# Expert 31's up matrix ahead of the second half of expert 30's down matrix, in a one-core hybrid layer with 32 experts

## What is computed

```
def clamped_swiglu(a, u):
    a = jnp.minimum(a, SWIGLU_LIMIT)
    u = jnp.clip(u, -SWIGLU_LIMIT, SWIGLU_LIMIT)
    return a * jax.nn.sigmoid(SWIGLU_ALPHA * a) * (u + 1.0)
...
    logits = (t @ router_w + router_b).astype(jnp.float32)
    top_v, top_i = lax.top_k(logits, TOP_K)
    gates = jax.nn.softmax(top_v, axis=-1)
...
    def expert_block(inp):
        tok, gt, e = inp
        xb = t_pad[tok]
        hid = clamped_swiglu(xb @ w_gate[e] + b_gate[e], xb @ w_up[e] + b_up[e])
        yb = hid @ w_down[e] + b_down[e]
        return (yb * gt[:, None].astype(yb.dtype)).astype(t.dtype)
```

## Time and profile before

| | us |
|---|---|
| median of 3 runs | 1059.69 (1058.49 to 1059.8) |
| the profiled execution's own time | 1057.99 |
| its span, first to last instruction | 1056.2 |
| TensorE busy | 1019.8 (97%) |
| VectorE busy | 228.7 (22%) |
| ScalarE busy | 143.8 (14%) |

### The profile page before, as it was taken

One profiled execution on the slowest core, in us unless ns is written; L12 is line 12 of the kernel. 1 busy time (PEld: TensorE's weight loads), 2 busy tenths in 40 slices (PEclk: granted clock), 3 DMA queues, 4 the chain that ended last, 5 costly groups with the idle time before them and its releaser, 6 DMA issues.

```text
span 1056.2 us, 12142 instructions
## 1 busy us (share of the span) xinstructions
PE 1019.8 (97%) x5116; PEld 448.6 (42%) x5116; DVE 228.7 (22%) x495; ACT 143.8 (14%) x348; POOL 30.6 (3%) x50
## 2 busy tenths in 40 slices
PE   8999999999999999999999999999999999999997
PEld 7888764333333333332333333333333333233332
DVE  5453652111111111111111112211111111111112
ACT  3312331111111111101110011111111111011102
POOL 1230100000000000000000000000000000000000
PEclk9999999999999999999999999999999999999999
DMA  9894889999999999999999999999999999999995
GB/s 314 274 412 191 267 314 357 432 426 436 431 429 430 433 432 431 431 434 432 431 431 434 431 429 430 431 433 430 431 428 434 432 432 429 434 426 426 428 419 238
DMA packets 40587, 426.21 MB, mean 404 GB/s; under 512 B 6986, under 2 KB 19411, under 8 KB 24036
## 3 DMA queue, kind: packets, MB, share of 16 engines
q1 hardware_dynamic: 38516, 424.12, 95.9%
q10 hardware_dynamic: 2032, 1.53, 0.6%
HBM read 424.59 MB, written 1.05 MB: 403 GB/s over the span
## 4 chain that ended last, share of the span: by engine, by line
PE 69%; DMA 29%; ACT 1%; DVE 0%; issue 0%; SPq 0%; POOL 0%; DVEq 0%; POOLq 0%; ACTq 0%
PE bank L1215 29%; DMA ring<-in_moe_w_up 18%; PE bank L1266 15%; DMA ring<-in_moe_w_gate 11%; PE bank L1195 4%; PE bank L1187 4%; PE bank L871 3%; PE bank L886 2%; PE bank L1061 2%; PE bank L1049 1%; PE bank L1003 1%; PE bank L1257 1%; PE bank L1135 1%; PE bank L964 1%; PE bank L1069 1%; PE bank L1235 1%
## 5 line engine op out<-in xcount | busy, mean ns | idle before, releaser
L1215 PE MATMUL bank<-ring,arena 128*64 128x512 f32 x1980 | 444.5, 601 | 24.5 <-DMA ring<-in_moe_w_up 20.7
L1215 PEld LDWEIGHTS bank<-ring,arena 128*64 128x64 f32 x1980 | 141.3, 138 | 297.3 <-issue 253.6
L1266 PE MATMUL bank<-ring,arena 128*64 128x512 f32 x1024 | 226.8, 595 | 1.5 <-issue 1.5
L1266 PEld LDWEIGHTS bank<-ring,arena 128*64 128x64 f32 x1024 | 71.5, 137 | 151.7 <-issue 150.1
L1663 DVE COPY arena<-bank 128x512 f32<-128x512 f32 x32 | 22.1, 692 | 326.1 <-PE bank L1266 326.1
L756 ACT ACTIVATE arena<-arena 128x512 f32<-128x512 f32 x32 | 20.1, 630 | 451.4 <-DVE arena L1650 451.4
L1195 PE MATMUL bank<-arena 64*128 64x512 f32 x256 | 72.0, 640 | 0.9 <-DVE arena L1663 0.9
L1187 PEld LDWEIGHTS bank<-arena 128*128 128x128 f32 x480 | 58.8, 196 | 22.8 <-issue 22.8
L1657 DVE TENSOR_SCALAR arena<-bank 128x512 f32<-128x512 f32 x32 | 22.1, 692 | 209.2 <-PE bank L1215 209.2
L767 ACT ACTIVATE arena<-bank 128x512 f32<-128x512 f32 x32 | 19.1, 597 | 336.3 <-PE bank L1257 336.3
L1187 PE MATMUL bank<-arena 128*128 128x128 f32 x480 | 64.5, 288 | 0.0
(11 more groups left out here) (281 smaller groups left out, 514.6 us busy)
## 6 DMA issues: line engine op xcount, KB each, us to landing
ring<-in_moe_w_down SPq DMA_DIRECT2D x25, 4096.0 KB, 28.3
ring<-in_moe_w_gate SPq DMA_DIRECT2D x24, 4096.0 KB, 24.7
ring<-in_moe_w_up SPq DMA_DIRECT2D x24, 4096.0 KB, 27.5
ring<-in_moe_w_down SPq DMA_DIRECT2D x10, 2048.0 KB, 16.6
ring<-in_moe_w_gate SPq DMA_DIRECT2D x9, 2048.0 KB, 21.4
ring<-in_moe_w_up SPq DMA_DIRECT2D x9, 2048.0 KB, 15.1
ring<-in_w_in SPq DMA_DIRECT2D x12, 1024.0 KB, 11.9
ring<-in_moe_w_gate SPq DMA_DIRECT2D x8, 1024.0 KB, 17.9
```

What stands on the lines that cost most here:

```text
L1215: ins = mm(b[h * SL:(h + 1) * SL, :], (xA[pp], xB)[q][:, k, par * SL:(par + 1) * SL], columns(unit_at(m, kt), h), start=False, stop=kt == ...
L1266: ins = mm(bank[6][h * SL:(h + 1) * SL, :], hidT[:, kt % 4, (kt // 4) * SL:(kt // 4 + 1) * SL], unit_at(2, kt)[:, h * 512:(h + 1) * 512], ...
```

## The change

Four edits, all around the last two experts:

- SP skips the second half of down of expert 30 at its place, and asks for it (line 446 of the changed kernel) behind the five pieces of up of expert 31, ahead of down of expert 31. It goes to the slot that it had before.
- TensorE multiplies the first half of down of expert 30 at its old place, then gate and up of expert 31, and only then the second half. Its weights, the hidden rows of expert 30, have a buffer of their own (`hidT30`).
- `scatter(30, 0)` and `scatter(30, 1)` move from either side of up of expert 31 to ahead of the first and behind the second of the eight row groups of its down. The transposes of `selG` go to bank 7 in tile 31, since bank 6 still holds half a sum.
- VectorE's copy of expert 30's result to `y_s` moves from the end of tile 30 to the end of tile 31, behind the last step of its hidden rows.

```diff
@@ SP @@
                         for rows, done in zip(HALVES, (landed[s], landed2[s])):
+                            if (e, m) == (NE - 2, 2) and rows is HALVES[1]:
+                                s30 = s
+                                continue
                             sp.dma_start(slot(s)[:, rows, :], piece_src(e, m, rows)).then_inc(done, 16)
                     elif isinstance(e, int) and e == NE - 1:
                         for c, rows in enumerate(map(slice, LAST_PIECES[m], LAST_PIECES[m][1:])):
                             sp.dma_start(slot(s)[:, rows, :], piece_src(e, m, rows)).then_inc(w_landed[LAST_AT[m] + c - 1] if c else landed[s], 16)
+                        if m == 1:
+                            sp.dma_start(slot(s30)[:, HALVES[1], :], piece_src(NE - 2, 2, HALVES[1])).then_inc(landed2[s30], 16)
@@ ScalarE @@
-                nc.scalar.activation(selGT[par], bank[6][:, 0:SEQ], ACT.Copy).then_inc(selGT_ok, 1)
+                b = bank[7] if isinstance(n, int) and n == NE - 1 else bank[6]
+                nc.scalar.activation(selGT[par], b[:, 0:SEQ], ACT.Copy).then_inc(selGT_ok, 1)
...
+                dst = hidT30 if isinstance(n, int) and n == NE - 2 else hidT
+                nc.scalar.activation(dst[:, :, :].rearrange("p c n -> p (c n)"), bank[4][:, :], ACT.Copy).then_inc(hidT_ok, 1)
@@ TensorE @@
+                def down(kts, hid, rows_at, here):
+                    for kt in range(KT)[kts]:
+                        here(2, kt)
+                        for h in range(2):
+                            ins = mm(bank[6][h * SL:(h + 1) * SL, :], hid[:, kt % 4, (kt // 4) * SL:(kt // 4 + 1) * SL],
+                                     rows_at(2, kt)[:, h * 512:(h + 1) * 512], start=kt == 0, stop=kt == KT - 1)
+                        if kt == KT - 1 or (kt + 1 in FIRST_PIECES[2] if first else kt == 3):
+                            ins.then_inc(d_ps if kt == KT - 1 else unit_used, 1)
...
-                if last:
-                    scatter(n - 1, 0, 1 - par)
                 hidden(1, bank[5], u_ok, u_ps)
...
                 if last:
-                    scatter(n - 1, 1, 1 - par)
+                    down(slice(4, 8), hidT30, rows_30, arrived_30)
                 pe.wait_ge(hid_ok, n + 1)
...
+                if last:
+                    scatter(n - 1, 0, 1 - par)
+                    pe.wait_ge(yd_ok, n)
+                    down(slice(0, 2), hidT, unit_at, arrived)
+                    scatter(n - 1, 1, 1 - par)
+                    down(slice(2, 8), hidT, unit_at, arrived)
+                elif isinstance(n, int) and n == NE - 2:
+                    down(slice(0, 4), hidT30, unit_at, arrived)
+                else:
+                    down(slice(0, 8), hidT, unit_at, arrived)
@@ VectorE @@
+                for of in {NE - 2: (), NE - 1: (NE - 2, NE - 1)}.get(n, (n,)) if isinstance(n, int) else (n,):
+                    dve.wait_ge(d_ps, of + 1)
+                    if not first:
+                        dve.wait_ge(scat[1], of)
+                    copy(y_s, bank[6][:, :]).then_inc(yd_ok, 1)
```

More of the change, by code:

```diff
@@ L148, in build @@
         hidT = cut(10368, 4, P)
+        hidT30 = cut(14272, 4, P)
         y_s = cut(12160, 512)
@@ L766, in tile @@
                     act.wait_ge(d_ps, n)
-                nc.scalar.activation(hidT[:, :, :].rearrange("p c n -> p (c n)"), bank[4][:, :], ACT.Copy).then_inc(hidT_ok, 1)
+                dst = hidT30 if isinstance(n, int) and n == NE - 2 else hidT
+                nc.scalar.activation(dst[:, :, :].rearrange("p c n -> p (c n)"), bank[4][:, :], ACT.Copy).then_inc(hidT_ok, 1)
                 if ahead is not None:
@@ L1197, in scatter, with tile @@
                 ins.then_inc(scat[t], 1)
-            def tile(n, par, first, unit_at, arrived, pp, gathers, scatters, late=None):
+            def tile(n, par, first, unit_at, arrived, pp, gathers, scatters, late=None, rows_30=None, arrived_30=None):
+                def down(kts, hid, rows_at, here):
[6 more added lines that the diff above has]
+                            ins.then_inc(d_ps if kt == KT - 1 else unit_used, 1)
                 def hidden(m, b, free, done):
@@ L1230, in tile @@
                     gate_transposes()
-                else:
+                last = isinstance(n, int) and n == NE - 1
+                if not first and not last:
                     pe.wait_ge(yd_ok, n)
@@ L1234, in tile @@
                 for t in range(NT):
-                    ins = tr(bank[6][:, t * P:(t + 1) * P], selG[:, par, t, :], ident[:, :])
+                    ins = tr(bank[7 if last else 6][:, t * P:(t + 1) * P], selG[:, par, t, :], ident[:, :])
                 ins.then_inc(selT_ps, 1)
@@ L1238, in tile @@
                     pe.wait_ge(list_ok, 1)
-                last = isinstance(n, int) and n == NE - 1
-                if last:
-                    scatter(n - 1, 0, 1 - par)
                 hidden(1, bank[5], u_ok, u_ps)
@@ L1312, in arrived, with rows_30, arrived_30 @@
                             pe.wait_ge(w_landed[u], 48 if u < 8 else 32)
+                    def rows_30(m, kt):
+                        return slot(ring_at(stage, UPE * (k - 1) + m) % RING)[:, kt, :]
+                    def arrived_30(m, kt):
+                        if kt == 4:
+                            pe.wait_ge(landed2[ring_at(stage, UPE * (k - 1) + m) % RING], (2 + UPE * UNROLL // RING) * 16)
                     first = isinstance(n, int) and n == 0
@@ L1319, in experts @@
                          (n + 2, it * (UNROLL // 2) + (k // 2 + 1), k % 2) if ahead else None, not first,
-                         n - LATE if isinstance(n, int) and n in (LATE, LATE + 1) else None)
+                         n - LATE if isinstance(n, int) and n in (LATE, LATE + 1) else None, rows_30, arrived_30)
                     if isinstance(n, int) and n == UNROLL - 1:
```

## The result

Seven executions of the changed kernel took 1061.84 to 1066.05 us, median 1063.83; seven of the kernel before 1058.17 to 1059.80, median 1059.13. The ratio is 1.0045, with a 95% interval of 1.0035 to 1.0056: slower, by 4.7 us between the medians.

What follows compares the result with a forecast made beforehand. TensorE and transfers were both taken as full, the end bounded by the last landing and the work behind it. 2.9 us for the later copy plus 1.5 for the clock, on 1059.69, gave 1064.1 us, range 1061.3 to 1066.3.

Steps and rivals of the forecast that it cites:

- The forecast's floor: At the end: behind a last landing at 1042.8 the copy can't start before 1043.9; reordering gains at most 0.2 us.
- The landings: Expert 31's gate and up land 5.0 us earlier, the moved half at 1032.8; down of expert 31 stays at 1042.8.
- TensorE up to the wait: Gate of expert 31 ends at 1020.42, up at 1028.7; TensorE then waits 4.1 us for the moved half.
- Behind the wait: From the half's landing at 1032.8 to the copy at 1047.0: 14.2 us of work, against 14.0 in the old order.
- The two terms: At the end: 2.9 us for the later copy, plus 1.5 us for a clock fall at the wait, 4.4 in sum.
- the rival with a second fall: Clock falls again after the 1.48 us gap behind the transposes: 2.9 + 3.4, 1066.0 us; counted in the forecast's case.
- two reasons: Behind up of expert 31: decisive landing is 1032.8, not 1030.0; scatters fill no 1.48 us wait, since scatter awaits `hidT_ok`.
- Wait without a fall: Rival: TensorE waits for the moved half but the clock does not fall; 1062.6 us, chance 0.18.
- land early: Rival: the moved half lands out of order, at 1028.7 TensorE doesn't wait; 1059.5 us, not slower, chance 0.11.
- its case: Wait for the moved half and fall of the clock: 1063.3 to 1066.4 us, chance 0.68.

Runs made afterwards that it cites:

- the version at 0.9997: Changed kernel with the moved half in four 0.5 MB pieces and expert 30's first scatter ahead of the wait for hidT_ok: 1058.72 us, ratio 0.9997.
- the second trace: The changed kernel run once more, unaltered, for a closer figure and another trace: 1064.14 us, ratio 1.0050 against the kernel before.
- the pieces: Changed kernel with the moved half asked for in pieces, each waited for by itself: two of 1 MB 1059.86 us, four of 0.5 MB 1059.46 us.
- the still later half: Changed kernel with the moved half asked for behind the first 1 MB of expert 31's down: 1066.16 us, ratio 1.0072.
- the scatters alone: Kernel before with only expert 30's two scatters moved among expert 31's down products, its down and copy at their old place: 1061.81 us, ratio 1.0028.
- the filler matmuls: Changed kernel with ten idle matmuls between up of expert 31 and the wait for the moved half: 1061.51 us, ratio 1.0028.

## Why the prediction was right

It named 1064.1 us in 1061.3 to 1066.3; the median is 1063.83. That the two are 0.3 us apart is partly luck: the forecast added 4.4 us to a median of 1059.69, and the measured rise was 4.7 over a median of 1059.13. What stands on record is the rise, and its two terms. Step by step:

- **What bounds the end.** The forecast's floor (copy not before 1043.9, with the last landing at 1042.8) was not contradicted, and not reached by any new version either. No version's ratio is clearly below 1; the lowest is 0.9997. But the last weights landed 6.3 us ahead of the copy in the changed kernel, and 1.6 us ahead of it in the version at 0.9997 (asked for at 1023.94, 19.5 us to landing, copy at 1045.04), where the forecast's floor is 1.1. That the stream's end, and not the order of the products, would stop a better order is argued and not shown.
- **The landings.** It had the moved half at 1032.8 and up's fifth row group at 1025.0; they came at 1032.5 and 1025.07. The last piece of down came at 1042.4, where 1042.8 was forecast. SP's queue cost nothing visible: the half was asked for 27.6 us ahead.
- **TensorE up to the wait.** Gate's end was put at 1020.42 (the selection's transposes start at 1020.44), up's at 1028.7 (32.52 less 3.79 is 28.73), the wait at 4.1 against 3.79.
- **Behind the wait.** 14.2 us from landing to copy were forecast; with the clock held up it is 14.47, the two row groups between the scatters taking 1.87 (1040.34 to 1042.21) instead of 1.73 and the half 3.58 instead of 3.5. With the low clock it is 16.17.
- **The two terms.** Traces give 2.9 for landing and order (4.61 less 1.70) and 1.70 for the clock in the profiled execution; 2.9 and 1.5 were forecast. That the clock falls at all had a chance of 8 in 10 in the forecast, and it fell in all three traces with a wait of 3.8 us or more. The clock's term was given 0 to 1.7 for one low stretch. In the second trace it was 2.55, above that bound but inside the 3.4 of the rival with a second fall. The rule of the Trainium skill (TensorE: Matmul & The Clock Gate, "HAM oscillation"), a wait for a transfer and a next burst that starts at half rate, agrees with two of the three traces that have the long wait (granted clock 0.50 from within the wait on). In the first one the burst's first 0.5 to 0.9 us were still at 1.00, and then it was 0.50 too.
- **Why the gain didn't come.** The text named two reasons. The later landing of the half has its runs in the pieces and in the still later half. That scatters among the down products don't fill the wait for `hidT_ok`, since they stand behind it, has one too: with the first scatter moved ahead of that wait, it is filled (0.5 us). What the text didn't price by itself is the scatters' move: it puts 2.1 us of work behind the landings (the scatters alone, by its trace).
- **The rivals.** Wait without a fall is what the filler matmuls make: 1061.51 against the 1062.6 named (the medians of before differ by 1 us; as a ratio 1.0028 against 1.0027). The half did not land early: up's pieces ahead of it, then the half, in the order of asking. A second fall is in none of the three traces with the long wait; its place as the dear case is taken by the one longer low stretch.
- **A slip in the sum.** 1059.69 plus 2.9, 3.4 and 0.3 is 1066.3, and not the 1066.4 that the text gives as the upper end of its case. The stated range isn't touched by it.

The size that no term explains is small: the scatters alone lose 0.9 us more by the ratio than in their trace.

## What to carry to other kernels

When a stream of transfers and an engine are both full, as here, the end is the last landing that is waited for plus the work queued behind it; so count, for each landing near the end, what stands behind it, and move work ahead of landings, not behind. A unit that must come late should come in pieces, each waited for by itself: a single semaphore for 2 MB made the engine stand 3.8 us, two pieces of 1 MB left 1.39 and 0.60, and four of 0.5 MB 0.2 to 0.9 at a time. And work moved to cover a wait covers nothing if the same wait is written ahead of it.

## What the runs showed of the hardware

- The clock's price for one and the same wait differs between executions: behind 3.79 and 3.77 us of idle TensorE the next sixteen rows took 5.35 and 6.20 us, against 3.65 at full clock. In the first the clock fell 0.5 to 0.9 us behind the wait's end, in the second within the wait.
- Whether this is also what makes the times spread is not shown. The changed kernel's lie 4.2 us apart (7 executions) and 2.9 (5), those of before 1.6 (7). But those with the filler matmuls lie 3.3 apart (7) and those of the scatters alone 3.1 (11), and neither has the long idle wait.
- Ten useless matmuls of 0.25 us each in a wait were worth 1.7 us to the work behind it (14.47 us from the landing to the copy, against 16.17).
- A fall of the clock behind a 2.11 us wait at 1003 us, in the run with filler matmuls, cost that execution nothing: TensorE was 2 us late at 1012 and was waiting for a landing again at 1033. Two executions lost 0.75 and 1.05 us to a fall in the last norm, at about 1051 us, behind which no wait is left to take it up.
